# Plain order of an expert pair in a two-layer MoE encoder kernel: gate products, activation, down products

## The chip, the cores and the metric

One core of one Trainium2 chip runs the whole program. The metric is the device time of one execution in microseconds (us). A reading of the profile gives the time of one execution, and the times of three unprofiled executions stand beside it.

## The reference, cut to what matters

Two layers work on 384 tokens of width 1024: 256 of a prompt and 128 of samples. Each layer is a mixer (attention and retention in layer 0, a convolution module in layer 1) and then a mixture of experts (MoE). The change is in the MoE alone. Everything is float32.

```python
def hier_moe(h, w_grp, b_grp, w_rexp, b_rexp, w_gate, w_up, w_down):
    ...
    for g in range(N_GROUPS):
        a = jnp.einsum('nd,edf->nef', x, w_gate[g])
        u = jnp.einsum('nd,edf->nef', x, w_up[g])
        hid = jax.nn.silu(a) * u * gates[:, g, :, None]
        out = out + jnp.einsum('nef,efd->nd', hid, w_down[g]).astype(F32)
```

There are 32 experts (4 groups of 8), each with three 1024 x 256 matrices. A token uses two of them; `gates` is zero elsewhere.

## The kernel before

**Pairs and windows.** The kernel takes the experts two at a time: 16 pairs (`NP`) in each layer. An expert gets a window of 64 tokens (`CAP`), so a pair fills 128 rows. Here no expert has more than 64 tokens and the loop over windows runs once in each layer.

**The weights of a pair.** A pair needs six loads of 1 MiB, numbered q = 6p to 6p + 5. The first four hold the gate and up matrices, the last two the down matrices. A layer has 96 loads, in two halves of 48 (`HALF`). They go into 20 slots in SBUF. `NEEDED` lists the load numbers of a half in the order in which they are loaded. `TURN` gives the slot position of each place in that order: 0 to 19, 0 to 19, then 5 to 12. So place 53, which is the sixth place of the second half, goes to position 5, and that position held place 40 before. `HOLDS` translates a position into a slot of SBUF, layer by layer, and `FREE` lists the slots in the order in which the mixer ahead gives them up; `FIRST` is the order of the first 20 loads that follows from it. I count the loads of a layer from 0 in the order in which they are loaded.

**The queues.** All expert loads are issued by SyncE (SP), in `expert_loads`. Before each load SP waits in `freed` until TensorE (PE) has used what lay in the slot: `gu_done` counts the gate and up products by load, `d_done` counts the down products by pair. SP's queue is in order, so a load that waits holds up all the later ones. GpSimd (POOL) gathers each pair's token rows from HBM (`gather`, into `XGT`) and scatters the results (`scatter`, from `Y` to `outs`). After the last pair SP loads `outs` back (`outs_back`), and VectorE (DVE) adds it to `X` (`add_back`). The result of the last pair isn't scattered: PE multiplies it with the transposed one-hot matrix (`combined`), and DVE adds that too (`add_last`).

**One pair on the engines.** PE makes the gate and up products (`gate_up`, two halves of 8 matmuls, each kept in the trace as two records). ACT applies silu (`silu`), DVE multiplies (`hidden`), PE transposes the result (`hidden_transposed`), ACT copies it to SBUF (`hidden_out`), PE makes the down products (`down`) and ACT scales them into `Y` (`y_out`). Beside that, PE transposes the rows of the next pair (`rows_transposed`), DVE copies them to `XG` (`rows_out`), and PE looks up the indices of the pair after next (`looked_up`).

**The order before.** PE is one pair behind with the down products: gate products of p, the next rows' transposes, a lookup, down products of p - 1, and then the transposes of the hidden values of p. Only the last pair differs: the down products of pair 14 come ahead of the gate products of pair 15, and those of pair 15 follow it. ACT and the loads have the same order, so `NEEDED` lists the gate loads of p ahead of the down loads of p - 1. The transposes for the window after the last pair, and DVE's copy of them, come at the very end of a window.

Of the kernel before, what the change touches and what calls it, by code (L numbers as in the profile page):

```python
# [42 lines left out]
NP = NE // 2  # L43
# [10 lines left out]
PE_TAPS = [r * NSTRIP for r in ROUNDS]  # L54
UNIT = 2048
LO, HI, SLOTS = 6, 12, 20
HOLDS = ((0, 1, 18, 19, 2, 10, 11, 12, 13, 14, 15, 16, 9, 3, 6, 7, 8, 17, 4, 5), (18, 19, 6, 7, 8, 9, 10, 11, 0, 1, 12, 13, 14, 15, 16, 17, 2, 3, 4, 5))
FREE = ((19, 18, 6, 7, 8, 17, 9, 16, 15, 14, 13, 12, 10, 11, 0, 1, 2, 3, 4, 5), (18, 19, 6, 7, 8, 9, 10, 11, 0, 1, 12, 13, 14, 15, 16, 17, 2, 3, 4, 5))
LOADS = 6 * NE // 2
HALF = LOADS // 2  # L60
NEEDED = [q for p in range(HALF // 6 - 1) for q in list(range(6 * p, 6 * p + 4)) + ([6 * p - 2, 6 * p - 1] if p else [])]
NEEDED += [HALF + n for n in (-8, -7, -6, -5, -4, -3, -2, -1)]
SKEW = 5
TURN = [*range(SLOTS), *range(SLOTS), *range(SKEW, SKEW + HALF - 2 * SLOTS)]
FIRST = [[NEEDED[holds.index(n)] for n in free] for holds, free in zip(HOLDS, FREE)]


def turn(q):

    return NEEDED.index(q % HALF)  # L70


def place(q):

    return TURN[turn(q)]


def laps(q):
# [3 lines left out]

def lap(q):

    return TURN[:turn(q)].count(place(q))


def held_before(q):

    n = next(n for n in range(turn(q) - 1, turn(q) - HALF - 1, -1) if TURN[n % HALF] == place(q))  # L90
    return NEEDED[n % HALF] + n // HALF * HALF


UNITS = NP + 2
# [131 lines left out]
def build(nc, a, o):  # L226

    with ExitStack() as ctx:
# [200 lines left out]
        def _(sp):  # L429
# [36 lines left out]

            def last_held(lay, n):

                return NEEDED[max(i for i in range(HALF) if HOLDS[lay][TURN[i]] == n)]

            def outs_back(lay, u):

# [6 lines left out]
            def expert_loads(lay, extra0):  # L479

                b, _ = layer_base(lay, extra0)
                for q in NEEDED[SLOTS:]:
                    freed(b, held_before(q))
                    expert_load(lay, q)
                sp.wait_ge(S("steps_known"), lay + 1)
                n = sp.value_load(NW[0:1, lay:lay + 1], min_val=0, max_val=MAXWIN - 1)
                with sp.Fori(1, n * 2 + 2) as half:
                    for q in NEEDED:
                        freed(b + half * (NP // 2), held_before(q))
                        expert_load(lay, q, half % 2)  # L490
                return n
# [181 lines left out]
        def _(pe):  # L673
# [386 lines left out]
            def moe(lay, extra0):  # L1060
# [145 lines left out]
                with pe.Fori(0, n + 1) as w:  # L1206
                    b, u = b0 + w * NP, u0 + w
                    for p in range(NP):
                        if p == NP - 1:
                            down(b, u, p - 1)  # L1210
                        gate_up(b, u, p, 0)
                        if p == 0:
                            looked_up(b, u, 0, 0, slice(0, 4))
                            looked_up(b, u, 1, 1, slice(0, 4, 3))
                            looked_up(b, u, 2, 2, slice(0, 4))
                        gate_up(b, u, p, 1)
                        if p + 1 < NP:
                            rows_transposed(b, u, p + 1)
                        if p:
                            looked_up(b, u, p + 2, p + 2, slice(0, 4) if p + 2 < NP else slice(1, 3))  # L1220
                        if p == NP - 3:
                            slots_transposed(u)
                        if 1 <= p < NP - 1:
                            down(b, u, p - 1)
                        hidden_transposed(b, p)
                    down(b, u, NP - 1)
                    rows_transposed(b, u, NP)
                combined(b0 + (n * NP + NP), u0 + (n + 1))
                if lay == 0:
                    x_transposed(1)  # L1230
# [102 lines left out]
        def _(act):  # L1333
# [151 lines left out]
            def moe(lay, extra0):  # L1485
                if lay:
                    preload(ACT.Sqrt)
                else:
                    fox_mixed(2)
                act.wait_ge(S("stored"), 16 * (STATE_STORES + lay * CONV_STORES))  # L1490
                gain = 2 * lay + 1
                for t in range(NT):
                    act.wait_ge(S("xt_done"), 2 * NT * lay + 2 * t + 1)
                    q.do(A(HM[:, 0:4, P * t:P * (t + 1)], PS[:, 4, :].rearrange("p (k n) -> p k n", n=P), ACT.Copy),
                         S("hm_act"))
                    act.wait_ge(S("x_mixed"), 2 * NT * lay + 2 * t + 2)
                    square(gain, t, XSQ[:, :])
                    rms(gain, t, t + 1)
                q.do(A(TB[:, :, :, 1], bc(C["tid"], 2, NE), ACT.Copy))
                act.wait_ge(S("rstd_ready"), (NT + 1) * (lay + 1))  # L1500
                q.do(A(TB[:, :, :, 2], bc(norms[:, gain, 6:9], 2, NE), ACT.Copy))
                q.settle()
                q.link(A(stat[:, 12:13], C["eps"], ACT.Copy), S("tb_ready"))
                preload(ACT.Exp)
                act.wait_ge(S("gl_centred"), 2 * lay + 1)
                q.link(A(E4[:, :, :], E4[:, :, :], ACT.Exp), S("gl_exp"))
                act.wait_ge(S("gl_centred"), 2 * lay + 2)
                q.link(A(R8[:, 21:24], R8[:, 18:21], ACT.Exp), S("gl_exp"))
                preload(ACT.Silu)

                def silu(b, u, p):

                    act.wait_ge(S("gu_done"), b * 4 + (4 * p + 4))
                    act.wait_ge(S("idx_read"), u * UNITS + (lay + 2 + p))
                    if p:
                        act.wait_ge(S("hid_ready"), b + p)
                    A(SG[:, :], PS[:, 2 + p % 2, 0:FE], ACT.Silu, scale=SC[:, p, 0:1]).then_inc(S("silu_ready"), 1)  # L1517

                def hidden_out(b, p):

                    act.wait_ge(S("hid_tr"), b + (p + 1))
                    A(HID[:, p % 2, :, :, :].rearrange("p j e n -> p (j e n)"), PS[:, 2 + p % 2, 0:FE], ACT.Copy  # L1522
                      ).then_inc(S("hidT_ready"), 1)

                def y_out(b, u, p):

                    act.wait_ge(S("d_done"), b + (p + 1))
                    act.wait_ge(S("idx_read"), u * UNITS + (lay + 2 + p))
                    if p:
                        act.wait_ge(S(f"scattered{p % 2}"), u * SENT + 16 * ((p + 1) // 2))  # L1530
                    A(Y[:, p % 2, :], PS[:, 4:6, :].rearrange("p a n -> p (a n)"), ACT.Copy,  # L1531
                      scale=SC[:, p, 1:2]).then_inc(S("y_ready"), 1)

                b0, u0 = layer_base(lay, extra0)
                act.wait_ge(S("steps_known"), lay + 1)
                n = act.value_load(NW[0:1, lay:lay + 1], min_val=0, max_val=MAXWIN - 1)
                with act.Fori(0, n + 1) as w:
                    b, u = b0 + w * NP, u0 + w
                    for p in range(NP):
                        if p == NP - 1:  # L1540
                            y_out(b, u, p - 1)
                        silu(b, u, p)
                        if 1 <= p < NP - 1:
                            y_out(b, u, p - 1)
                        hidden_out(b, p)
                    y_out(b, u, NP - 1)
                    for parity in range(2):
                        act.wait_ge(S(f"scattered{parity}"), u * SENT + SENT)
                return n
# [67 lines left out]
        def _(dve):  # L1617
# [312 lines left out]
            def moe(lay, extra0):  # L1930
# [64 lines left out]
                with dve.Fori(0, n + 1) as w:  # L1995
# [4 lines left out]
                    index_out(u, 2, 2, slice(0, 2), slice(0, 2))  # L2000
                    for p in range(NP):
                        hidden(b, p)
                        if p + 1 < NP:
                            rows_out(b, p + 1)
                        if 1 <= p < NP - 2:
                            index_out(u, p + 2, p + 2, slice(0, 2), slice(0, 2))
                        elif p:
                            index_out(u, p + 2, p + 2, slice(1, 2), slice(0, 1))
                        if p == NP - 3:
                            dve.wait_ge(S("gt_tr"), u + 1)  # L2010
                            V.tensor_copy(GT[:, :], PS[:, 6, 0:TOK]).then_inc(S("gt_ready"), 1)
                            V.tensor_scalar(SV[:, :, :], SV[:, :, :], float(-CAP), None, ALU.add).then_inc(S("sv_moved"), 1)
                            dve.wait_ge(S("sv_moved"), u + 1)
                        if p + 1 < NP:
                            onehot(u, p + 3)
                    rows_out(b, NP)

                def add_back(t):

# [176 lines left out]
```

## Time and profile before

| | |
|---|---|
| median of 3 executions | 925.65 us (924.63 to 926.55) |
| the profiled execution | 927.78 us, of which the span shown is 926.0 us |
| PE matmul busy | 863.5 us (93%) |
| DVE, ACT, POOL busy | 337.3 us (36%), 213.6 us (23%), 93.5 us (10%) |
| moved by DMA | 276.91 MB, mean 299 GB/s |
| mean granted TensorE clock | 0.99 of full speed |
| MoE of layer 0 | about 254 to 487 us of the span |
| MoE of layer 1 | about 690 to 923 us of the span |

PE's busy share says little here, since matmuls are pipelined and their ends are modelled. The DMA rate by stretch tells more: the chain that ended last has expert loads and SP's queue in it, with 13% and 8% of the span.

### The profile page before, as it was taken

The page shows a single profiled execution, that of the slowest core. Times are in us where ns is not written, and L with a number is a line of the kernel's source. Part 1 is how long each engine was busy: PE and PEld are TensorE (multiplying, and loading weights), DVE is VectorE, ACT ScalarE, POOL GpSimd, SP SyncE. Part 2 cuts the span into 40 slices and gives each one's busy share as a digit, 9 for nine tenths or more (in the row PEclk, how much of TensorE's full clock was granted, in tenths as well). Part 3 has the DMA queues.
Part 4 walks back from the last instruction along what each step waited for, and adds up shares of the span by engine and source line. Part 5 has one row for each costly group of instructions (what it writes and reads, how often), then busy time and mean ns, then how long its engine had stood idle before and what let it go on. Part 6 is the DMA issues. An engine that isn't in the chain of part 4 may idle for free.

```text
span 926.0 us, 14125 instructions
## 1 busy us (share of the span) xinstructions
PE 863.5 (93%) x5406; PEld 492.9 (53%) x5406; DVE 337.3 (36%) x809; ACT 213.6 (23%) x464; POOL 93.5 (10%) x110
## 2 busy tenths in 40 slices
PE   8999999999999999978778999989999999988775
PEld 6888888888843333322235555447973333333222
DVE  1521653433631111111053689983262111101105
ACT  4322233522211111111123123335121111111010
POOL 1400000000021111101100000000011111111110
PEclk9999999999999999999997999999999999999998
DMA  9972720595889998999999521043559998999995
GB/s 356 414 269 68 213 103 1 219 414 213 345 336 417 405 419 345 419 419 418 419 393 421 201 92 70 23 120 146 204 198 395 418 411 361 395 417 418 420 418 232
DMA packets 49730, 276.91 MB, mean 299 GB/s; under 512 B 11304, under 2 KB 11456, under 8 KB 20920
## 3 DMA queue, kind: packets, MB, share of 16 engines
q1 hardware_dynamic: 35472, 244.94, 65.7%
q0 software_dynamic: 13616, 30.02, 9.4%
q10 hardware_dynamic: 576, 1.05, 0.3%
q8 instruction: 44, 0.72, 0.3%
q14 instruction: 22, 0.18, 0.1%
HBM read 267.62 MB, written 31.66 MB: 323 GB/s over the span
## 4 chain that ended last, share of the span: by engine, by line
PE 66%; DMA 14%; SPq 8%; DVE 7%; issue 2%; ACT 2%; DVEq 0%; ACTq 0%
PE PS L1131 13%; DMA slot<-in_experts 13%; PE PS L700 13%; PE PS L1256 9%; SPq L457 8%; PE PS L1155 7%; PE PS L960 7%; PE PS L937 2%; PE PS L1109 2%; DVE X L1622 2%; PE PS L1275 2%; PE PS L1066 1%; PE PS L1097 1%; DVE YC L2099 1%; DMA HT<-in_x_feat 1%
## 5 line engine op out<-in xcount | busy, mean ns | idle before, releaser
L1131 PE MATMUL PS<-slot,XG 128*64 128x512 f32 x1024 | 233.6, 598 | 28.9 <-DMA slot<-in_experts 28.6
L1131 PEld LDWEIGHTS PS<-slot,XG 128*64 128x64 f32 x1024 | 69.3, 136 | 170.2 <-issue 137.6
L1952 DVE SCALAR_TENSOR_TENSOR hid_by_token<-PS,SC,SG 128x256 f32<-128x256 f32 x32 | 15.5, 484 | 348.5 <-ACT SG L1517 344.7
L700 PE MATMUL PS<-slot,HT 128*128 128x256 f32 x576 | 131.4, 383 | 1.0 <-ACT HT L1357 1.0
L1155 PE MATMUL PS<-slot,HID 128*64 128x512 f32 x512 | 116.6, 597 | 3.5 <-ACT HID L1522 3.5
L700 PEld LDWEIGHTS PS<-slot,HT 128*128 128x128 f32 x576 | 107.3, 190 | 19.2 <-ACT HT L1357 3.3
L1256 PE MATMUL PS<-HC,slot 128*128 128x384 f32 x256 | 88.9, 504 | 1.6 <-DVE HC L2048 1.6
L1256 PEld LDWEIGHTS PS<-HC,slot 128*128 128x128 f32 x256 | 49.0, 195 | 41.7 <-issue 11.8
L1517 ACT ACTIVATE SG<-PS,SC 128x256 f32<-128x256 f32 x32 | 15.2, 475 | 233.1 <-PE PS L1131 233.1
L1531 ACT ACTIVATE Y<-PS,SC 128x1024 f32<-128x1024 f32 x32 | 35.7, 1115 | 139.6 <-PE PS L1155 139.6
L1155 PEld LDWEIGHTS PS<-slot,HID 128*64 128x64 f32 x512 | 33.5, 137 | 60.4 <-issue 53.5
L618 POOL DMA_INDIRECT XGT<-rows,IDX x34 | 34.9, 1025 | 301.2 <-DVE SC L1945 238.5
L1961 DVE TENSOR_TENSOR XG<-PS,small 128x512 f32<-128x512 f32 x68 | 43.7, 682 | 10.6 <-PE PS L1109 10.2
L2099 DVE SCALAR_TENSOR_TENSOR YC<-U,small,YC 128x384 f32<-128x384 f32 x74 | 45.1, 610 | 0.0
L960 PE MATMUL PS<-slot,YC 128*128 128x256 f32 x192 | 42.2, 379 | 0.4 <-ACT YC L1611 0.4
L1109 PEld LDWEIGHTS PS<-cst,XGT 128*128 128x128 f32 x256 | 27.5, 141 | 26.3 <-issue 21.4
L2099 DVE SCALAR_TENSOR_TENSOR YD<-U,small,YD 128x384 f32<-128x384 f32 x66 | 40.2, 610 | 0.0
L960 PEld LDWEIGHTS PS<-slot,YC 128*128 128x128 f32 x192 | 36.2, 190 | 5.8 <-issue 1.0
L626 POOL DMA_INDIRECT outs<-Y,IDX x30 | 30.2, 1008 | 85.1 <-ACT Y L1531 68.3
L1109 PE MATMUL PS<-cst,XGT 128*128 128x128 f32 x256 | 34.9, 279 | 0.2 <-DMA XGT<-rows,IDX 0.2
L1374 ACT ACTIVATE PJ<-PS,norms 128x256 f32<-128x256 f32 x36 | 16.9, 474 | 77.9 <-PE PS L700 77.5
L1275 PE MATMUL PS<-U,DG 32*32 32x384 f32 x736 | 22.5, 505 | 3.0 <-ACT stat L1579 3.0
(308 smaller groups left out, 825.4 us busy)
## 6 DMA issues: line engine op xcount, KB each, us to landing
slot<-in_experts SPq DMA_DIRECT2D x192, 1024.0 KB, 16.1
slot<-in_w_pw SPq DMA_DIRECT2D x12, 1024.0 KB, 9.9
slot<-in_w_in SPq DMA_DIRECT2D x11, 1024.0 KB, 12.1
outs<-slot POOLq DMA_DIRECT2D x12, 512.0 KB, 10.1
slot<-outs SPq DMA_DIRECT2D x6, 1024.0 KB, 8.1
slot<-in_w_out SPq DMA_DIRECT2D x4, 1024.0 KB, 7.3
rows<-X POOLq DMA_DIRECT2D x6, 512.0 KB, 8.6
KTC<-in_k_past POOLq DMA_DIRECT2D x1, 2048.0 KB, 13.8
```

The lines of the kernel that those rows point to most:

```text
L457: sp.dma_start(slot[HOLDS[lay][place(q)]][:, :], experts[bass.ds(half * HALF + (lay * LOADS + q), 1), :, :].rearrange("o p n -> p (o n)")) ...
L618: pool.indirect_dma_start(XGT[:, p % 2, :], None, rows[lay], bass.IndirectOffsetOnAxis(IDX[:, p % NP, 1:2], 0), bounds_check=TOK - 1, oob_ ...
L700: last = mm(PS[:, in_bank(n), 0:UCOL], HT[:, k, P * t:P * (t + 1)], w[:, k, :], start=k == 0, stop=k == KD - 1)
L960: last = mm(PS[:, RING[i % 4], UCOL * (u % 2):UCOL * (u % 2) + UCOL], lhs[:, k, P * t:P * (t + 1)], w[:, k, :], start=k == 0, stop=k == ks ...
L1109: last = nc.tensor.transpose(PS[:, k // 4, P * (k % 4):P * (k % 4 + 1)], XGT[:, p % 2, P * k:P * (k + 1)], ident)
L1131: last = mm(PS[CAP * e:CAP * (e + 1), 2 + p % 2, :], XG[:, p % 2, k, CAP * e:CAP * (e + 1)], w[:, k % 2, e, :], start=k == 0, stop=k == KD ...
L1155: last = mm(PS[CAP * e:CAP * (e + 1), 4 + n, :], HID[:, p % 2, j, e, :], w[:, e, 512 * n:512 * (n + 1)], start=j == 0, stop=j == 1, skip_g ...
L1256: last = mm(PS[:, 2 * (c % 2) + g, 0:TOK], w[:, k, P * cc:P * (cc + 1)], HC[:, k, :], start=k == 0, stop=k == KD - 1)
L1275: last = mm(PS[STRIP * j:STRIP * (j + 1), 4 + i, 0:TOK], DG[rows, c % 2, w, :], U[rows, c, :, w:w + LS], start=m == 0, stop=m == ROUNDS[c] ...
L1531: A(Y[:, p % 2, :], PS[:, 4:6, :].rearrange("p a n -> p (a n)"), ACT.Copy, scale=SC[:, p, 1:2]).then_inc(S("y_ready"), 1)
L1961: V.tensor_tensor(XG[:, p % 2, 4 * h:4 * h + 4, :], PS[:, h, :].rearrange("p (k n) -> p k n", n=P), bc(GC[:, gain, 4 * h:4 * h + 4], 2, P) ...
L2099: ins = V.scalar_tensor_tensor(acc, src, tap, acc, ALU.mult, ALU.add)
```

## The change

PE, ACT and DVE now treat each pair in plain order. On PE these are gate products of p, the transposes of the rows of p + 1, the lookup, the hidden transposes of p and the down products of p. On ACT `y_out` of p follows `hidden_out` of p. The loads go by number, so that `NEEDED` and `turn` are gone, and `HOLDS` of layer 0 is renumbered. For the last pair the row transposes for a following window, and DVE's copy of them, now stand inside the pair and no longer at the end.

```diff
-HOLDS = ((0, 1, 18, 19, 2, 10, 11, 12, 13, 14, 15, 16, 9, 3, 6, 7, 8, 17, 4, 5), (18, 19, 6, 7, 8, 9, 10, 11, 0, 1, 12, 13, 14, 15, 16, 17, 2, 3, 4, 5))
+HOLDS = ((0, 1, 18, 19, 2, 9, 10, 11, 12, 13, 14, 15, 16, 3, 4, 5, 6, 7, 8, 17), (18, 19, 6, 7, 8, 9, 10, 11, 0, 1, 12, 13, 14, 15, 16, 17, 2, 3, 4, 5))
...
-NEEDED = [q for p in range(HALF // 6 - 1) for q in list(range(6 * p, 6 * p + 4)) + ([6 * p - 2, 6 * p - 1] if p else [])]
-NEEDED += [HALF + n for n in (-8, -7, -6, -5, -4, -3, -2, -1)]
...
-FIRST = [[NEEDED[holds.index(n)] for n in free] for holds, free in zip(HOLDS, FREE)]
+FIRST = [[holds.index(n) for n in free] for holds, free in zip(HOLDS, FREE)]
...
-                for q in NEEDED[SLOTS:]:
+                for q in range(SLOTS, HALF):
                     freed(b, held_before(q))
                     expert_load(lay, q)
...
                     for p in range(NP):
-                        if p == NP - 1:
-                            down(b, u, p - 1)
                         gate_up(b, u, p, 0)
...
                         gate_up(b, u, p, 1)
-                        if p + 1 < NP:
-                            rows_transposed(b, u, p + 1)
+                        rows_transposed(b, u, p + 1)
...
-                        if 1 <= p < NP - 1:
-                            down(b, u, p - 1)
                         hidden_transposed(b, p)
-                    down(b, u, NP - 1)
-                    rows_transposed(b, u, NP)
+                        down(b, u, p)
...
                     for p in range(NP):
-                        if p == NP - 1:
-                            y_out(b, u, p - 1)
                         silu(b, u, p)
-                        if 1 <= p < NP - 1:
-                            y_out(b, u, p - 1)
                         hidden_out(b, p)
-                    y_out(b, u, NP - 1)
+                        y_out(b, u, p)
...
                         hidden(b, p)
-                        if p + 1 < NP:
-                            rows_out(b, p + 1)
+                        rows_out(b, p + 1)
...
-                    rows_out(b, NP)
```

On PE, at pair 7 of layer 0, this stands before. L1131 are gate products, L1109 the row transposes, L1097 the lookup, L1155 down products and L1140 the hidden transposes; the first number in a slot's name is its slot in SBUF.

```order
L1131 MATMUL PS<-slot12_69,XG_114 64x512 x4
L1131 MATMUL PS<-slot13_70,XG_114 64x512 x4
L1126 REGISTER_ALU
L1131 MATMUL PS<-slot14_71,XG_114 64x512 x4
L1131 MATMUL PS<-slot15_72,XG_114 64x512 x4
L1109 MATMUL PS<-cst_50,XGT_119 128x128 x8
L1084 REGISTER_ALU
L396 REGISTER_ALU
L1097 MATMUL PS<-TB_130,G_115 64x4 x6
L1155 MATMUL PS<-slot10_67,HID_133 64x512 x4
L1155 MATMUL PS<-slot11_68,HID_133 64x512 x4
L1140 MATMUL PS<-cst_50,hid_by_token_132 128x128 x2
```

And this stands there after the change, from the end of pair 6 to the end of pair 7's gate products and row transposes (here L1123 are gate products, L1101 row transposes, L1132 hidden transposes, L1147 down products).

```order
L1132 MATMUL PS<-cst_50,hid_by_token_132 128x128 x2
L1109 REGISTER_ALU
L1147 MATMUL PS<-slot9_66,HID_133 64x512 x4
L1147 MATMUL PS<-slot10_67,HID_133 64x512 x4
L1118 REGISTER_ALU
L1123 MATMUL PS<-slot11_68,XG_114 64x512 x4
L1123 MATMUL PS<-slot12_69,XG_114 64x512 x4
L1118 REGISTER_ALU
L1123 MATMUL PS<-slot13_70,XG_114 64x512 x4
L1123 MATMUL PS<-slot14_71,XG_114 64x512 x4
L1101 MATMUL PS<-cst_50,XGT_119 128x128 x8
```

The down products of pair 6 used to follow pair 7's gate products and now precede them. They use the loads of places 40 and 41, and those slots take places 53 and 54 next.

On DVE, at the end of layer 0's MoE, this stands before: the last `hidden`, the last index, the copy of the rows for a following window (XG), and then the additions to X.

```order
L1952 SCALAR_TENSOR_TENSOR hid_by_token_132<-PS,SC_136,SG_116 128x256
L1942 REGISTER_ALU
L1944 TENSOR_SCALAR IDX_135<-PS 128x1
L1945 COPY SC_136<-PS 128x1
L1958 REGISTER_ALU
L1960 REGISTER_ALU
L1961 TENSOR_TENSOR XG_114<-PS,small_51 128x512
L1960 REGISTER_ALU
L1961 TENSOR_TENSOR XG_114<-PS,small_51 128x512
```

After the change it is this.

```order
L1934 SCALAR_TENSOR_TENSOR hid_by_token_132<-PS,SC_136,SG_116 128x256
L1940 REGISTER_ALU
L1942 REGISTER_ALU
L1943 TENSOR_TENSOR XG_114<-PS,small_51 128x512
L1942 REGISTER_ALU
L1943 TENSOR_TENSOR XG_114<-PS,small_51 128x512
L1924 REGISTER_ALU
L1926 TENSOR_SCALAR IDX_135<-PS 128x1
L1927 COPY SC_136<-PS 128x1
```

The two copies have moved ahead of the last index. What PE does for them, the row transposes, stood behind the last down products and now stands between the last gate products and the last hidden transposes.

## Rows read from the trace of the kernel before

**Rows 1.** Windows: PE, PEld, DVE, ACT, POOL busy us, granted clock, DMA share, GB/s.
```profile
350.00:360.00 10.00, 10.00 (x56) 3.71 (x52) 0.41 (x2) 1.87 (x3) 1.94 (x2) 1.00 0.78 280
780.00:790.00 10.00, 10.00 (x62) 3.90 (x60) 2.28 (x6) 1.86 (x3) 2.01 (x2) 1.00 0.64 238
400.00:460.00 60.00, 49.21 (x255) 16.51 (x252) 8.97 (x25) 8.10 (x12) 8.30 (x9) 1.00 1.02 419
```
**Rows 2.** DMA queue of the loads, 270 to 345 us, then 705 to 780 us.
```profile
q1 hardware_dynamic: 3958, 28.83, 93.1%
...
q1 hardware_dynamic: 4022, 29.29, 94.2%
```
**Rows 3.** The chain that ended last: start us, us, what.
```profile
265.31 7.09 PE PS L1131 x32
...
273.87 3.48 PE PS L1155 x16
277.73 7.02 PE PS L1131 x32
...
348.03 3.48 PE PS L1155 x16
...
700.25 7.09 PE PS L1131 x32
...
782.87 3.49 PE PS L1155 x16
```
**Rows 4.** Timeline of SP: start us, us, line, operation.
```profile
256.74 5.45 SPq L457 DMA_DIRECT2D slot<-in_experts  x3
...
351.70 3.33 SPq L457 DMA_DIRECT2D slot<-in_experts  x6
...
786.54 4.33 SPq L457 DMA_DIRECT2D slot<-in_experts  x6
```
**Rows 5.** Timeline around the first pair and the last pair of layer 0.
```profile
264.71 0.44 PE L1140 MATMUL PS<-cst,hid_by_token 128*128 128x128 f32 x2 [0.15 <-DVE hid_by_token L1952]
...
466.45 1.94 PE L1131 MATMUL PS<-slot,XG 128*64 128x512 f32 x8 [0.77 <-DMA slot<-in_experts]
...
469.62 0.44 PE L1140 MATMUL PS<-cst,hid_by_token 128*128 128x128 f32 x2 [0.93 <-DVE hid_by_token L1952]
470.09 0.38 ACT L1522 ACTIVATE HID<-PS 128x256 f32<-128x256 f32 x1 [1.05 <-PE PS L1140]
470.53 3.65 PE L1155 MATMUL PS<-slot,HID 128*64 128x512 f32 x16 [0.47 <-ACT HID L1522]
```
**Rows 6.** Timeline behind the last pair of layer 0, then of layer 1.
```profile
474.81 1.29 DVE L1961 TENSOR_TENSOR XG<-PS,small 128x512 f32<-128x512 f32 x2 [5.11 <-PE PS L1109]
...
475.57 5.41 PE L1176 MATMUL PS<-Y,GT 128*128 128x512 f32 x12 [0.36 <-ACT Y L1531]
476.01 4.99 DVE L1622 TENSOR_TENSOR X<-X,slot 128x1024 f32<-128x1024 f32 x4
...
911.59 4.99 DVE L1622 TENSOR_TENSOR X<-X,slot 128x1024 f32<-128x1024 f32 x4
```
**Rows 7.** SP's loads of `outs`: first issue in each layer (timeline), their DMA lines.
```profile
468.70 1.42 SPq L476 DMA_DIRECT2D slot<-outs  x3
slot<-outs SPq DMA_DIRECT2D x1, 1024.0 KB, 5.3
slot<-outs SPq DMA_DIRECT2D x1, 1024.0 KB, 7.5
...
903.02 1.41 SPq L476 DMA_DIRECT2D slot<-outs  x3
slot<-outs SPq DMA_DIRECT2D x1, 1024.0 KB, 6.5
```
**Rows 8.** DMA issues of the page: the scatters, count, median us to landing.
```profile
outs<-Y,IDX POOLq DMA_INDIRECT x32, 8.0
```

More of the change, by code:

```diff
@@ L60 @@
 HALF = LOADS // 2
-NEEDED = [q for p in range(HALF // 6 - 1) for q in list(range(6 * p, 6 * p + 4)) + ([6 * p - 2, 6 * p - 1] if p else [])]
-NEEDED += [HALF + n for n in (-8, -7, -6, -5, -4, -3, -2, -1)]
 SKEW = 5
 TURN = [*range(SLOTS), *range(SLOTS), *range(SKEW, SKEW + HALF - 2 * SLOTS)]
-FIRST = [[NEEDED[holds.index(n)] for n in free] for holds, free in zip(HOLDS, FREE)]
-def turn(q):
-    return NEEDED.index(q % HALF)
+FIRST = [[holds.index(n) for n in free] for holds, free in zip(HOLDS, FREE)]
 def place(q):
-    return TURN[turn(q)]
+    return TURN[q % HALF]
 def laps(q):
@@ L83, in lap @@
 def lap(q):
-    return TURN[:turn(q)].count(place(q))
+    return TURN[:q % HALF].count(place(q))
 def held_before(q):
-    n = next(n for n in range(turn(q) - 1, turn(q) - HALF - 1, -1) if TURN[n % HALF] == place(q))
-    return NEEDED[n % HALF] + n // HALF * HALF
+    return next(n for n in range(q - 1, q - HALF - 1, -1) if place(n) == place(q))
 UNITS = NP + 2
@@ L467, in last_held @@
             def last_held(lay, n):
-                return NEEDED[max(i for i in range(HALF) if HOLDS[lay][TURN[i]] == n)]
+                return max(q for q in range(HALF) if HOLDS[lay][place(q)] == n)
             def outs_back(lay, u):
@@ L487, in expert_loads @@
                 with sp.Fori(1, n * 2 + 2) as half:
-                    for q in NEEDED:
+                    for q in range(HALF):
                         freed(b + half * (NP // 2), held_before(q))
```

## The prediction, on record before the run

> **What bounds the kernel now.** I read the rate of the DMA engines by stretch first. In the second half of layer 0's MoE it stands at 419 GB/s with a DMA share of 1.02, while PE is busy for 49 of 60 us [rows 1]: the loads set the pace there, and PE waits for them. The same holds in layer 1. In the first half PE has a lead of 20 loads and never waits for one. Its pace is even: from the down products at 273.87 us to those at 348.03 us it makes six pairs in 74.2 us, 12.36 us a pair [rows 3]. The loads are slower. The queue of the loads moved 28.83 MB in 75 us, so that a load of 1.0486 MB takes 2.73 us and a pair's six take 16.4 us [rows 2]. In layer 1 it is 2.69 us and 16.1 us [rows 2].
>
> A stage bound by loads ends earlier only if the stream starts earlier, has fewer holes, or if less stands behind it. So I looked for holes. There is one in each layer: 350 to 360 us moved only 280 GB/s and 780 to 790 us only 238 GB/s [rows 1]. Against 418 GB/s that is 10 x (1 - 280/418) = 3.3 us and 4.3 us without data. In both cases SP ends the hole with a burst of six issues, at 351.70 and 786.54 us [rows 4], right behind down products that end at 348.03 + 3.48 = 351.5 us and 782.87 + 3.49 = 786.4 us [rows 3]. These are the down products of pair 6. The first load of the burst is load 53; its slot held load 40, a down load of pair 6. The distance is 13 loads there, where elsewhere it is 15 to 28. So the hole is made by the slot order, and by the fact that PE does the down products of pair 6 only after pair 7's gate products.
>
> **The change part by part.** Term 1, PE's pace. Nothing is added to PE's work, but a wait is exposed. Between the hidden transposes and what follows there stood gate products, which waited for nothing; these came 0.38 us after the end of the down products (277.73 less 273.87 + 3.48) [rows 3]. Now the down products follow, and they need ACT's copy. The last pair already runs this way: transposes at 469.62, copy at 470.09, down products at 470.53 us, which is 0.91 us from start to start [rows 5]. Silu and DVE's product lie under the row transposes and the lookup, since the hidden transposes could start 469.62 - 468.39 = 1.2 us behind the last gate product [rows 5], and the other two take longer than that (the down products start 1.5 us behind gate products that end at 272.40) [rows 3]. So a pair takes 12.36 + 0.91 - 0.38 = 12.9 us. This is still 3.3 us under the loads' 16.1 to 16.4 us, and the cover for it is the lead of 20 loads: no cost of its own.
>
> Term 2, when down slots come free. The first hidden transposes start at 264.71 us [rows 5]; down 0 then starts at 265.6 and ends at 269.2 us. Down p ends at 269.2 + 12.9 p. For pair 6 that is 346.7 us, against 351.5 now. Layer 1's second pair starts 434.94 us later (700.25 less 265.31) [rows 3], which gives 704.2 us for down 0 and 781.6 us for down 6, against 786.4. The slot comes 4.8 us earlier, and the holes are 3.3 and 4.3 us: both close. I take 3.3 + 4.3 = 7.6 us. The Trainium skill ("DMA: Bandwidth & Descriptors", "Specifications") gives about 358 GB/s as a core's HBM limit. The trace runs at 419 GB/s here, so I go by the trace; with 358 as the full rate the holes would be 2.2 and 3.4 us and the total gain 8.7 us.
>
> Term 3, new holes. In plain order loads 24 and 25 wait for down 0, and loads 43 and 44 for down 4; before they waited for gate products and for the down products of pair 3 and gate products. Let a load's data start 1 us behind its issue (my estimate). The stream then wanted load 53 at 351.7 + 1 - 3.3 = 349.4 us, load 43 ten loads before, at 322.1, and load 24 at 270.2 us. After the change these can flow at 320.8 + 1 = 321.8 and at 270.2 us: on the edge. In layer 1 load 53 was wanted at 783.2, load 43 at 756.4 and load 24 at 705.3 us, and they can flow at 756.8 and 705.2 us: 0.4 us late. Bounds: nothing if the issue is faster than that, and 1.6 us a layer if the first four refills, issued from 256.74 us [rows 4], flow at full rate (257.7 + 4 x 2.73 = 268.6, against 270.2). I charge 0.5 and 0.4 us, and as a delay of the stream they are one charge a layer. Terms 2 and 3 give 6.7 us.
>
> Term 4, behind the last load. DVE now copies the rows of a following window (1.29 us) behind PE's last work, and only then, at 476.01 us, adds what SP loads back [rows 6]. But the first block lands at 468.70 + 5.3 = 474.0 us and the second at about 469.13 + 7.5 = 476.6 us [rows 7], the second being issued 0.43 us after the first. With the copy moved into the pair, the four additions run as 474.0 to 476.5 and 476.6 to 479.1 us and end 1.9 us before today's 481.0 [rows 6]. In layer 1 the first block lands at 903.02 + 6.5 = 909.5 us [rows 7]; the additions end at 914.5 us and not at 911.59 + 4.99 = 916.6 [rows 6]: 2.1 us. Bounds: nothing if the landings move as late as DVE, and 2.0 and 2.1 us if DVE starts the moment the first block is there. On PE the row transposes (1.1 us) now stand ahead of the last hidden transposes. Together with the lookup they take 1.5 us where the chain needs 1.2, so the last down products come 0.3 us later; the last products with Y start at 475.9 instead of 475.57 us and DVE wants the first of them at 479.1. That is hidden. Term 4 is 4.0 us.
>
> Nothing else counts. The first 20 loads are the same number in the same slots and land before the first gate product. ACT's order has `y_out` directly behind the down products, ahead of the next silu, which is 7 us away. SP passes through the same number of waits. POOL's gathers and scatters keep their order; a scatter's data is ready some 12 us earlier.
>
> Sum: 7.6 - 0.9 + 4.0 = 10.7 us. The profiled execution took 927.78 us (span 926.0 and 1.8 around it), 2.1 us above the median. Its successor should show 917.1 us, and the median goes from 925.65 to 914.9, say 915.0 us. A measurement of this kernel tells 0.2%, 1.9 us, from no change.
>
> **The rivals.** (a) The holes close only by half: the gap of 13 loads is still the tightest place, and 0.4 us in layer 1 are no margin. For it speaks that three places (24, 43, 53) come within a microsecond of the stream. Against it, 4.8 us gained on a wait of 3.3. With half of 7.6 and the 0.9 charge the gain is 6.9, so 918.8 us, and 921 us with 1.6 us a layer lost as well. Chance 0.16.
>
> (b) The tails give nothing, since the landings or the last products hold DVE. For it speaks that in layer 1 all three blocks come only within DVE's reach of the end. Gain 6.7 us, 918.9 us. Chance 0.12.
>
> (c) Nothing to be measured: the stream's rate, not its holes, gives back what the holes cost, because packets only run more densely with the scatters. Against it, the rate stands at 413 to 419 GB/s on either side of each hole. 925 us. Chance 0.05.
>
> (d) Slower, by ACT's queue. `y_out` of p waits until the scatter of p - 2 has landed, and it now stands ahead of silu of p + 1, so that a late scatter stops PE's whole chain. POOL issues the scatter of p - 2 behind a gather, by my estimate 4.5 us after pair p - 1's gate products (the lookup at 1.0, DVE's index and the gather behind it). With 8.0 us to landing [rows 8] it is there 12.5 us after them, and `y_out` of p wants it at 12.9 + 5.9 = 18.8 us. It decides when a landing takes over 14.3 us, and beyond that each microsecond is one more on a pair. At 14.0 us a pair down 6 ends at 353.2 us, each layer loses 2 us and the tails' 4.0 are used up. At 15 us a pair it is 8 us a layer: 925.65 + 16 - 4 = 938 us. Chance 0.05.
>
> (e) Slower, by PE's clock. PE now stops in every pair, where it ran from 265 to 390 us without a stop. Where it stops far more today, the granted clock is 1.00, which is 2.4 GHz, with 11 us idle in 60 [rows 1]. The Trainium skill ("TensorE: Matmul & The Clock Gate", "Why this matters for your kernels") warns that idle gaps between bursts bring the clock down; new gaps of 0.5 us are far shorter than those today. At 1.2 GHz a pair would take 25.8 us. If pairs 0 to 6 ran so, load 53 would come 85 us later, some 1090 us in all. Chance 0.02.
>
> **How the numbers follow.** My forecast, 911.5 to 918 us, has 0.60. Cases (a) and (b) lie at 918 to 921 us on the same side. The range is 911.5 to 920.5: it leaves out the slow cases and no change (0.12), and some 0.08 at the two ends. Faster: 0.60 + 0.16 + 0.12 = 0.88. Same 0.05, slower 0.07.
>
> **What the profile would show.** Right: about 12.9 us between pairs in the first half, down products of pair 6 that end at 347 and 4.7 us earlier in layer 1, no stretch of 10 us under 360 GB/s between 265 and 440 us, PE waiting for loads only from pair 13 on instead of pair 10, and DVE's additions to X starting before PE's last down products end. Wrong: a hole at about 268 us or 320 us, a pair of 13.5 us or more, silu waiting behind `y_out`, or additions to X that start as late after the last load as today.

## The result, and the profile after

The changed kernel takes 916.55 us (median of 4, 914.61 to 918.94), the kernel before 926.1 us (median of 4, 924.63 to 927.42). The ratio is 0.9898, with a 95% interval of 0.9867 to 0.993: 9.4 us faster, by at least 6.5. Ratios here and below are taken over each kernel's undisturbed executions, and the only one left out is an execution of E6 that took 2812.07 us, for which no trace shows a cause. The forecast was 915.0 us in a range of 911.5 to 920.5. The profiled execution took 918.94 us with a span of 917.2, which is 8.8 us under its predecessor, where I had written 10.7.

The windows that answer to [rows 1] (PE, PEld, DVE, ACT, POOL busy us, granted clock, DMA share, GB/s):

```profile
350.00:360.00 10.00, 9.53 (x60) 4.01 (x58) 2.27 (x6) 1.56 (x3) 2.01 (x2) 1.00 1.02 425
780.00:790.00 10.00, 9.53 (x58) 3.88 (x56) 2.27 (x6) 0.95 (x3) 2.02 (x2) 1.00 1.01 420
400.00:460.00 60.00, 52.95 (x293) 19.97 (x291) 9.77 (x26) 7.90 (x12) 9.27 (x9) 1.00 1.02 417
```

280 and 238 GB/s have become 425 and 420, and 770 to 780 us, where layer 1's hole would now lie, moves 419: both holes are gone. Two windows ahead of layer 0's hole changed as well. First the kernel before, then the changed one:

```profile
310.00:320.00 10.00, 10.00 (x62) 3.71 (x61) 2.28 (x6) 1.57 (x3) 2.02 (x2) 1.00 0.99 387
340.00:350.00 10.00, 10.00 (x62) 3.94 (x60) 2.28 (x6) 1.16 (x3) 1.09 (x2) 1.00 0.93 381
```

```profile
310.00:320.00 10.00, 9.53 (x59) 3.84 (x56) 2.28 (x6) 0.86 (x2) 1.71 (x2) 1.00 1.03 420
340.00:350.00 10.00, 9.45 (x58) 4.07 (x58) 2.28 (x6) 1.97 (x3) 2.02 (x2) 1.00 1.02 418
```

So the kernel before lost another 0.7 and 0.9 us there, which the prediction didn't count. Next comes the chain that ended last, at the first pair and at pair 6 (down products in L1147, gate products in L1123, row transposes in L1101, hidden transposes in L1132):

```profile
265.60 3.65 PE PS L1147 x16
269.26 6.87 PE PS L1123 x32
276.12 1.02 PE PS L1101 x8
277.15 0.45 PE PS L1089 x12
277.60 0.38 PE PS L1132 x2
278.00 0.39 ACT HID L1508
278.44 3.65 PE PS L1147 x16
282.09 6.87 PE PS L1123 x32
...
342.69 3.65 PE PS L1147 x16
346.34 6.87 PE PS L1123 x32
```

From 269.26 to 282.09 a pair takes 12.83 us, and 12.36 before [rows 3]. Pair 6's down products end at 346.3 us, not at 351.5. The timeline of SP shows load 53 issued right behind them, at 346.52 us, where it stood at 351.70 [rows 4]:

```profile
346.52 5.48 SPq L449 DMA_DIRECT2D slot<-in_experts  x5
```

The end of layer 0's MoE, in the timeline (XG is the copy that was moved, L468 are the loads of `outs`):

```profile
462.23 1.94 PE L1123 MATMUL PS<-slot,XG 128*64 128x512 f32 x8 [1.07 <-DMA slot<-in_experts]
...
465.26 1.28 DVE L1943 TENSOR_TENSOR XG<-PS,small 128x512 f32<-128x512 f32 x2
...
466.48 3.65 PE L1147 MATMUL PS<-slot,HID 128*64 128x512 f32 x16 [0.47 <-ACT HID L1508]
...
466.57 1.42 SPq L468 DMA_DIRECT2D slot<-outs  x3
...
471.44 2.48 DVE L1604 TENSOR_TENSOR X<-X,slot 128x1024 f32<-128x1024 f32 x2 [4.77 <-DMA slot<-outs]
```

The copy is out of DVE's way, as it should be. But DVE now waits 4.77 us for the landing of `outs`. SP asks for `outs` 4.3 us after the last gate products begin (462.23); before it was 2.3 us (468.70 less 466.45) [rows 5, 7]. The end of layer 1:

```profile
893.23 1.94 PE L1123 MATMUL PS<-slot,XG 128*64 128x512 f32 x8 [1.10 <-DMA slot<-in_experts]
...
896.60 1.41 SPq L468 DMA_DIRECT2D slot<-outs  x3
...
902.59 2.48 DVE L1604 TENSOR_TENSOR X<-X,slot 128x1024 f32<-128x1024 f32 x2 [4.92 <-DMA slot<-outs]
```

What `outs` waited for is in the chain that ended last. In layer 0 it no longer goes through the last gate products. It runs from the down products of pair 14 (L1147) over their scatter (`outs<-Y,IDX`) to SP's request and the landing of the second block:

```profile
450.95 3.67 PE PS L1147 x16
...
456.95 9.60 DMA outs<-Y,IDX
466.57 0.40 SPq L468
467.01 7.03 DMA slot<-outs
474.13 1.24 DVE X L1604
```

### The profile page after: what moved, and what is told of

It is laid out like the page before. It is cut to its first block, busy times and chain, and to the rows that moved or that the text cites. A ratio compares the mean times of both kernels' runs of the same rounds, so it can differ in the third digit from the quotient of the medians.

```text
span 917.2 us, 14121 instructions
## 1 busy us (share of the span) xinstructions
PE 859.1 (94%) x5406; PEld 498.6 (54%) x5406; DVE 337.2 (37%) x809; ACT 216.6 (24%) x464; POOL 93.4 (10%) x110
## 4 chain that ended last, share of the span: by engine, by line
PE 65%; SPq 12%; DMA 11%; DVE 7%; ACT 3%; issue 2%; DVEq 0%; ACTq 0%; POOLq 0%
PE PS L692 13%; PE PS L1123 12%; SPq L449 11%; PE PS L1242 9%; PE PS L1147 7%; PE PS L952 7%; DMA slot<-in_experts 6%; PE PS L929 2%; DMA outs<-Y,IDX 2%; DVE X L1604 2%; PE PS L1101 2%; PE PS L1261 2%; DMA slot<-outs 2%; PE PS L1058 1%; PE PS L1089 1%
## 5 line engine op out<-in xcount | busy, mean ns | idle before, releaser
L1123 PE MATMUL PS<-slot,XG 128*64 128x512 f32 x1024 | 229.2, 594 | 12.7 <-DMA slot<-in_experts 12.7
L1123 PEld LDWEIGHTS PS<-slot,XG 128*64 128x64 f32 x1024 | 72.6, 137 | 160.7 <-issue 143.8
L1147 PE MATMUL PS<-slot,HID 128*64 128x512 f32 x512 | 116.9, 598 | 15.4 <-ACT HID L1508 15.4
L1147 PEld LDWEIGHTS PS<-slot,HID 128*64 128x64 f32 x512 | 34.0, 136 | 77.8 <-issue 57.0
L1101 PEld LDWEIGHTS PS<-cst,XGT 128*128 128x128 f32 x256 | 27.5, 141 | 26.0 <-issue 23.5
L1101 PE MATMUL PS<-cst,XGT 128*128 128x128 f32 x256 | 35.0, 280 | 0.0
```

Source lines behind the costliest of these rows:

```text
L1101: last = nc.tensor.transpose(PS[:, k // 4, P * (k % 4):P * (k % 4 + 1)], XGT[:, p % 2, P * k:P * (k + 1)], ident)
L1123: last = mm(PS[CAP * e:CAP * (e + 1), 2 + p % 2, :], XG[:, p % 2, k, CAP * e:CAP * (e + 1)], w[:, k % 2, e, :], start=k == 0, stop=k == KD ...
L1147: last = mm(PS[CAP * e:CAP * (e + 1), 4 + n, :], HID[:, p % 2, j, e, :], w[:, e, 512 * n:512 * (n + 1)], start=j == 0, stop=j == 1, skip_g ...
```

## The experiments

Theory A: the holes are waits for slots, and PE's order of the pair closed them. Theory B: the additions at the end are held by `outs`, whose loads wait for the scatter of pair 14, and the moved copy gives next to nothing. Rival C: the order of the loads did it. Rival D: the hole is a stall of the chip's own.

**E1, the changed kernel again.** 

> The changed kernel once more, as the measure for the runs beside it. All theories: 0.990 of the kernel before, 916 to 917 us. Theory A (release): the down products of pair 6 end near 346.3 us and no 10 us stretch from 265 to 440 us falls under 360 GB/s. Theory B (end): the first block of outs lands some 9.2 us after the last gate load of a layer is there, and DVE's additions to X begin on that landing in both layers.

918.08 us (6 runs), ratio 0.9894 (0.987 to 0.9918). Pair 6's down products end at 346.25 us, no 10 us window from 270 to 440 us moves less than 370 GB/s, and DVE's additions wait for the landing of `outs` in both layers, 9.2 and 8.8 us after the last gate products begin. Both parts hold.

**E2, plain engines, old load order.** PE, ACT and DVE as in the change; `NEEDED`, `turn` and `HOLDS` as before.

> PE, ACT and DVE in plain order, but the loads in the old order (gate loads of p ahead of the down loads of p - 1). Theory A, that the holes closed because PE frees pair 6's down slots earlier: down 6 ends near 346.5 us, the holes at 350 and 780 us are closed, the time is that of the changed kernel within 1.5 us, 915 to 918 us. Rival C, that the gain comes from loading by number: the holes stay or most of the 9.4 us is lost, 922 us or more.

924.71 us (10 runs), ratio 0.9974 (0.9955 to 0.9994). By time the rival was right, and the time is 6.7 us above the range that I gave theory A. By place it wasn't: the old holes did close, with 418 GB/s from 350 to 360 us. But there are new ones. From its first refill (the first load that takes over the slot of an earlier load of the layer) E2 moves 26.71 MB in 70 us and the changed kernel 27.66; in layer 1 it is 26.52 and 27.59 MB. At 418 GB/s that is 2.3 and 2.6 us. The largest is from 270 to 280 us, with 317 GB/s against 365: in the old list place 24 waits for gate products of pair 1, which plain PE makes only after the down products of pair 0. The rest of the loss, some 2.5 us of 7.4, is at the end. The timeline of E2 from 448 us (L1155 down, L1131 gate products):

```profile
448.09 1.94 PE L1155 MATMUL PS<-slot,HID 128*64 128x512 f32 x8 [0.46 <-DMA slot<-in_experts]
449.85 7.04 PE L1131 MATMUL PS<-slot,XG 128*64 128x512 f32 x32
459.28 3.65 PE L1155 MATMUL PS<-slot,HID 128*64 128x512 f32 x16 [0.55 <-ACT HID L1516]
462.76 7.04 PE L1131 MATMUL PS<-slot,XG 128*64 128x512 f32 x32
472.11 3.65 PE L1155 MATMUL PS<-slot,HID 128*64 128x512 f32 x16 [0.47 <-ACT HID L1516]
```

The down loads of pair 13 come behind the gate loads of pair 14, and plain PE wants them first. When they are there at 448 us, all of pair 14's and most of pair 15's gate work is still to be done at PE's own pace. The last down products end at 475.8 us, against 470.1 in the changed kernel.

**E3, the copy back at the end.**

```diff
-                        rows_transposed(b, u, p + 1)
+                        if p + 1 < NP:
+                            rows_transposed(b, u, p + 1)
...
                         down(b, u, p)
+                    rows_transposed(b, u, NP)
...
-                        rows_out(b, p + 1)
+                        if p + 1 < NP:
+                            rows_out(b, p + 1)
...
+                    rows_out(b, NP)
```

> The changed kernel with the row transposes for a following window, and DVE's copy of them, back behind the last down products. My prediction's term 4 (DVE's copy held up the additions, 1.9 and 2.1 us): 4 us slower than the changed kernel, near 920.5 us. Theory B (the landing of outs holds them since the change, and the copy is hidden): within 0.5 us of the changed kernel, additions start 0 to 0.4 us later against the last gate load.

916.65 us (4 runs), ratio 0.9897 (0.9866 to 0.9928); E1 on the same chip has 0.9894. My term 4 falls: 4 us more would have been 0.994. The timeline of DVE in both layers:

```profile
470.12 1.29 DVE L1945 TENSOR_TENSOR XG<-PS,small 128x512 f32<-128x512 f32 x2 [5.11 <-PE PS L1101]
471.33 2.48 DVE L1606 TENSOR_TENSOR X<-X,slot 128x1024 f32<-128x1024 f32 x2
...
898.87 1.29 DVE L1945 TENSOR_TENSOR XG<-PS,small 128x512 f32<-128x512 f32 x2 [5.11 <-PE PS L1101]
900.08 2.47 DVE L1606 TENSOR_TENSOR X<-X,slot 128x1024 f32<-128x1024 f32 x2
```

Its last gate products begin at 461.77 and 890.52 us. The additions begin 9.56 us after them in both layers, exactly as in the kernel before (476.01 - 466.45) [rows 5, 6]. In the changed kernel it is 9.21 and 9.36 us. So the start of the additions moves by 0.35 and 0.2 us. Their end moves less, since the second block is late: in layer 0 the first four are done 14.4 us after the last gate products begin, and 14.6 us in E3 and in the kernel before. From the last gate products of layer 1 to the end of the span it is 24.0 us in all three.

**E4, the old order for pairs 13 and 14.** Built on E2, with the changed kernel's `HOLDS`:

```diff
+NEEDED = [*range(HALF - 14), *range(HALF - 12, HALF - 8), HALF - 14, HALF - 13, *range(HALF - 8, HALF)]
...
+                        if p == NP - 2:
+                            down(b, u, p - 1)
                         hidden_transposed(b, p)
-                        down(b, u, p)
+                        if p != NP - 3:
+                            down(b, u, p)
```

and the same for `y_out`.

> Plain order for pairs 0 to 12 and 15, the old order for pairs 13 and 14 on PE and ACT, with the gate loads of pair 14 ahead of the down loads of pair 13 (in both halves of the load list). Theory B, that the scatter of pair 14 comes too late in plain order and holds outs back: SP's first load of outs is issued about 2.2 us after the last gate products begin (changed kernel: 4.3 and 3.4 us after them in layers 0 and 1), DVE's additions begin 1.5 to 1.9 us earlier against them in each layer, 913 to 915 us. If another thing binds the end, such as the rate of the three blocks, it is 916 to 917 us as the changed kernel.

917.78 us (6 runs), ratio 0.9894 (0.9864 to 0.9923): no gain over the changed kernel, and above the 913 to 915 us that I expected. The relation that I forecast is there, but not for the reason that I gave. The timeline in layer 0:

```profile
464.72 1.94 PE L1130 MATMUL PS<-slot,XG 128*64 128x512 f32 x8 [0.57 <-DMA slot<-in_experts]
...
467.15 1.42 SPq L475 DMA_DIRECT2D slot<-outs  x3
...
472.51 1.23 DVE L1617 TENSOR_TENSOR X<-X,slot 128x1024 f32<-128x1024 f32 x1 [3.36 <-DMA slot<-outs]
```

SP asks for `outs` 2.4 us after the last gate products begin, and DVE starts 7.8 us after them. But these begin later themselves. From the first refill (258.16 us here, 256.72 in the changed kernel) it is 206.6 us, against 205.5 there and 206.1 in E1; from the first refill to the additions 214.4 and 214.7. Counted so, the scatter of pair 14 isn't any earlier: POOL issues it at 458.53 us here and at 456.95 in the changed kernel, 200.4 and 200.2 us after the first refill. It lands in 8.6 us and not 9.6, so SP asks for `outs` about 0.9 us sooner; the rest of what looks like a gain is that the gate products are late. The windows (columns as above) show what was traded. First the changed kernel, then E4:

```profile
465.00:467.00 2.00, 1.53 (x20) 0.87 (x20) 1.67 (x5) 0.38 (x1) 0.00 (x0) 1.00 0.42 172
467.00:468.00 1.00, 1.00 (x8) 0.39 (x6) 0.00 (x0) 0.00 (x0) 0.46 (x1) 1.00 0.55 66
```

```profile
467.00:469.00 2.00, 1.53 (x23) 1.10 (x20) 1.66 (x4) 0.69 (x2) 0.00 (x0) 1.00 0.65 195
```

Ahead of `outs` the changed kernel has a gap of 2 x (1 - 172/418) + (1 - 66/418) = 2.0 us; E4 has 1.1. More flows ahead of the last gate products in E4: 84.64 MB from 257.4 us on, against 84.33 MB from 256 us on in the changed kernel, or 0.7 us at 418 GB/s. Of these 0.31 MB, 0.09 are on the queue of the gathers and scatters, so pair 14's scatter, which here has more time to flow ahead of the last gate load, is at most a part of it; no run isolates it.

**E5, old engines, loads by number.** With the changed kernel's `HOLDS`.

```diff
-NEEDED = [q for p in range(HALF // 6 - 1) for q in list(range(6 * p, 6 * p + 4)) + ([6 * p - 2, 6 * p - 1] if p else [])]
-NEEDED += [HALF + n for n in (-8, -7, -6, -5, -4, -3, -2, -1)]
+NEEDED = list(range(HALF))
```

> The old order on PE, ACT and DVE, but the loads by number. Theory A (PE's order sets the release, the order of loads doesn't): down 6 still ends near 351.5 us, both holes stay at 3 to 4 us, 925 to 928 us. Rival C (the order of the loads is what gained): holes gone or smaller, 920 us or less.

935.38 us (4 runs), ratio 1.0106 (1.0075 to 1.0136): slower than the kernel before. Rival C is out as the sole cause, though E2 shows that the loads' order is needed too. My own expectation missed as well: the late hole did go, but because a bigger one came first. The windows:

```profile
268.00:272.00 4.00, 4.00 (x22) 1.34 (x18) 0.00 (x0) 0.00 (x0) 0.00 (x0) 1.00 0.58 230
272.00:280.00 8.00, 8.00 (x54) 3.26 (x52) 2.27 (x6) 1.86 (x3) 1.01 (x1) 1.00 0.24 63
...
350.00:360.00 10.00, 10.00 (x54) 3.67 (x52) 0.39 (x1) 1.87 (x3) 1.96 (x2) 1.00 1.02 418
```

Load 24 waits for down 0, which old PE does behind pair 1's gate products; they end at 277.5 us. 8.6 us are lost there, and the stream is so late from then on that load 53 finds its slot free.

**E6 to E8, the place of the extra laps.** `SKEW` shifts the eight positions that a half uses a third time; `HOLDS` swaps two slots along with it.

```diff
-SKEW = 5
+SKEW = 6
```

> The kernel before with SKEW 6 in place of 5: the eight extra loads of a half go one position further on, so that load 54 and not load 53 is the first to wait for pair 6's down products, and loads 40 and 41 wait for those of pair 3 (distances 14 and 14 in place of 15 and 13). Theory A: the hole at 350 us goes, a small one of 1.5 to 2 us appears near 314 and 749 us; net 4 us faster than before, near 922 us. Rival D, that the hole is a stall of the chip (HBM or queue) at the change of halves and not a wait for a slot: the hole stays in its place and the time is 926 us.

922.38 us (5 runs), ratio 0.9948 (0.993 to 0.9966): 4.8 us faster than before, by the place of the extra laps alone. Windows at 315 and at the old hole:

```profile
310.00:320.00 10.00, 10.00 (x62) 3.71 (x61) 2.28 (x6) 1.57 (x3) 2.02 (x2) 1.00 0.80 295
350.00:360.00 10.00, 10.00 (x56) 3.71 (x52) 0.42 (x2) 1.86 (x3) 1.93 (x2) 1.00 1.02 418
```

The hole at 350 us is gone, and the one at 310 to 320 us has grown from 387 to 295 GB/s, that is from 0.7 to 10 x (1 - 295/418) = 2.9 us; I had expected 1.5 to 2. In layer 1 it is the same, with 414 GB/s from 780 to 790 us and 295 from 740 to 750. The hole goes where the wait for a slot goes. Rival D is out.

> The changed kernel with SKEW 6: loads 42 and 43 now wait for pair 4's down products and are wanted at 319.5 us, where these end at 320.6. Theory A: a hole of 2 to 2.5 us near 320 us and the same near 750 us, 4 to 5 us slower than the changed kernel, near 921 us. Rival D: no change, 916 to 917 us.

920.77 us (10 runs), ratio 0.9944 (0.9924 to 0.9963). The window at the new hole of layer 0:

```profile
316.00:326.00 10.00, 9.53 (x51) 3.36 (x50) 1.67 (x5) 1.50 (x2) 2.02 (x2) 1.00 0.95 339
```

The whole of it lies between 310 and 326 us, where E7 moves 355 GB/s and the changed kernel 418; in layer 1 it is 361 and 414 GB/s from 740 to 760 us. The holes are 16 x (1 - 355/418) = 2.4 us and 20 x (1 - 361/418) = 2.7 us. Against E1's 0.9894 (another chip, each against the kernel before beside it) the kernel is 0.5% slower, some 4.6 us. As expected.

> The changed kernel with SKEW 4: load 52 in place of 53 waits for pair 6's down products (distance 12). Theory A: load 52 is wanted at about 346.5 us and can flow at 347.5, a hole of about 1 us a layer, 1 to 3 us slower than the changed kernel, 917.5 to 919.5 us. Rival D: no change.

919.37 us (4 runs), ratio 0.9924 (0.9903 to 0.9945); 0.3% above E1, but the two intervals overlap, so the time alone doesn't tell it from the changed kernel. The hole does. From 345 to 351 us it moves 367 GB/s and the changed kernel 416: 0.7 us in layer 0, where I had expected about 1. Pair 6's down products are hardly a microsecond ahead of the stream, and load 53 is the first that can wait for them.

**E9, small matmuls against a falling clock.** 4 + 9 + 3 matmuls of 128 columns whose results nothing reads, at three places between layer 0's MoE and the convolution, for instance

```diff
                     x_transposed(2)
+                    for _ in range(9):
+                        mm(PS[:, 3, TOK:TOK + P], cst[:, 0:P], cst[:, 0:P], start=True, stop=True, skip_group_check=True)
```

> The changed kernel with 16 small matmuls on PE whose results nothing reads: 4 behind layer 0's last products with Y, 9 while PE waits for the third tile of X, 3 ahead of the matmuls for the row scales. Theory E: the granted clock fell to 0.5 at 484 us because PE was idle for half of 476 to 484 us, and the first convolution matmuls then ran slow until 494 us; with the small matmuls the clock stays at 1.00 (or falls later and for less), and the convolution stage, from its first to its last glu product, takes 109.1 us and not 112.1: 3 us faster than the changed kernel, near 914 us, and less scatter between executions. Rival: the clock falls anyhow, as the small matmuls don't fill enough: 917 to 918 us, or 0.5 us slower by what they delay.

917.72 us (6 runs), ratio 0.9895 (0.9868 to 0.9921). The clock did what was expected; the median didn't. The trace shows what became of the time. Layer 1's first refill is issued at 683.86 us, 3.5 us before the changed kernel's 687.32, but its last gate products begin at 892.30 us, only 0.9 us before 893.23. Between the two 85.26 MB flowed, against 84.40, and 0.86 MB are 2.1 us at 418 GB/s: the mixer was done earlier, and more of the loads was still to come.

**E10, the changed kernel beside E9.** 

> The changed kernel, beside e9 on the same chip: 0.990 of the kernel before, 916 to 918 us, executions spread over some 4 us, the shorter ones with a mean clock of 0.995 and the longer ones with 0.991.

916.62 us (6 runs, 916.57 to 917.35), ratio 0.9887 (0.9868 to 0.9905). The spread that I expected was not there. Windows of the changed kernel, of E9 and of E10, from 484 to 492 us:

```profile
484.00:492.00 8.00, 5.61 (x18) 3.52 (x16) 5.34 (x14) 0.87 (x3) 0.00 (x0) 0.52 1.02 422
```

```profile
484.00:492.00 8.00, 6.21 (x32) 4.38 (x30) 5.82 (x15) 1.11 (x4) 0.00 (x0) 1.00 1.01 421
```

```profile
484.00:492.00 8.00, 6.45 (x27) 5.20 (x27) 4.83 (x13) 1.61 (x4) 0.00 (x0) 0.80 1.02 422
```

And the first convolution matmuls in the chain (64 records), in the same order:

```profile
488.66 23.81 PE PS L1242 x64
```

```profile
488.18 20.88 PE PS L1248 x64
```

```profile
489.17 20.88 PE PS L1242 x64
```

The granted clock at 0.52 costs 2.9 us there. E9 avoids it, but E10, without small matmuls, had its fall earlier and was back at the full clock before these began. In E10 too the gain shrinks in layer 1, from 2.5 us at the first refill (684.81) to 1.3 at the last gate products (891.89). No version beats the changed kernel beyond the intervals.

## Why the prediction was right, step by step

**Term 1, PE's pace: right.** 12.83 us a pair against 12.9 forecast, down 0 ending at 269.3 against 269.2, down 6 at 346.3 against 346.7. The exposed copy was read from the last pair before, the only one that ran in plain order already.

**Term 2, the holes close: right and shown, but undersized.** They are gone in the profile, E6 moves the hole with the slot order alone, and E7 and E8 open new ones: 2.4 and 0.7 us in layer 0, where the same two lines (when a down product ends, when the stream wants its slot) gave 2 to 2.5 and 1. E6's was 2.9 and not 1.5 to 2. The reading of the holes was narrow: one window of 10 us each. Layer 0 had 0.7 us more from 310 to 320 us and 0.9 us from 340 to 350. With 381 GB/s ahead of the hole (and 407 behind it in layer 1), my sentence in rival (c) that the rate stands at 413 to 419 on either side was a wrong reading. The assumption that a load's data start 1 us behind its issue fits the trace: load 53 is issued at 351.70 us, and the first packets of that queue come between 352.5 and 352.7.

**Term 3, new holes: too small, within its bound.** In layer 0, 260 to 270 and 270 to 280 us moved 388 and 413 GB/s before and 381 and 365 after, which is 1.3 us; I charged 0.5 and bounded it at 1.6.

**Terms 2 and 3 together were too small.** I forecast 2.8 and 3.9 us. The last gate products begin 4.2 us earlier in layer 0 (466.45 to 462.23) and 8.8 in layer 1 (902.02 to 893.23). Layer 1's first refill is 4.3 us early (691.65 to 687.32), which leaves 4.5 for layer 1. That is 8.7 and not 6.7 us. Besides the holes that I hadn't counted, less flows ahead of these products: from 256 us on 84.67 MB before and 84.33 MB after, in layer 1 from its first refill on 84.77 and 84.40 MB, which is 0.8 and 0.9 us at 418 GB/s. For layer 0 that makes 3.3 + 1.6 - 1.3 + 0.8 = 4.4 us, against 4.2 measured. E4 agrees: with the old order of the last pairs 84.64 MB flow, and these products come 0.5 to 1.1 us later, counted from the first refill.

**Term 4, the copy: wrong.** 4.0 us forecast, 0.2 us measured in layer 0 and nothing in layer 1. The step that failed is "the first block lands at 474.0", which I held fixed against the last loads. SP waits for the scatter of pair 14 before it asks for `outs`, and in plain order pair 14's gate loads come two loads later in the list. Counted from the layer's first refill, the last gate products came 4.2 and 4.5 us earlier, but that scatter was issued only 3.0 and 3.1 us earlier (before at 459.98 and 895.09, after at 456.95 and 887.64) and took 9.6 and 9.0 us to land, where it had taken about 8.7 and 7.9. So SP's request moved by 2.1 us in both layers. Two of the signs that I had named turned against the forecast here: the additions start nearly as late after the last load as before, and at 471.44 us they are behind the end of PE's last down products (466.48 + 3.65 = 470.1), not ahead of it. I had named "nothing, if the landings move as late as DVE" as the lower bound and rival (b) for this case; it came true while the loads gained 2 us more than I had summed. Two errors of about +2 and -4 us partly cancel. That 916.6 us lies so near to 915.0 is in part luck; the mechanism of the holes isn't.

**The rivals.** (a) and (c) didn't occur. (b) did, as a mechanism. (d): from 262 to 470 us ACT waits for PE alone and never for a scatter; PE's waits from 262 to 460 us are 7.2 us for ACT's copy in 15 pairs, the 0.48 us a pair that term 1 had priced, and 5.1 us for loads. (e): from 262 to 470 us the granted clock stays at 1.00, which is 2.4 GHz. It wasn't out of reach: in E2, where PE waits up to 3.2 us at a time for down loads, it was 0.78 from 390 to 400 us and 0.84 from 430 to 440, while the loads kept their 420 and 414 GB/s.

**That the change would need both of its halves** I had not said. The engines' order alone gives 0.3%, the loads' order alone costs 1.1%, both together gain 1.0%.

## What to carry to other kernels

In a stage bound by loads, look for windows in which the rate falls, and ask which slot the first load behind the gap waited for; the price is the time by which the stream wants the slot before its user is done, and both can be written as lines over the pairs. Load order, use order and slot release are one design: here the engines' order alone gained 0.3%, the loads' order alone cost 1.1%, and both together gained 1.0%. Read a hole from its edges and not from one round window, or part of it is missed. Work that is moved off the end pays only if the next thing in line, here a landing, isn't late itself, so move it on paper together with all that precedes it. And count both from a common event, such as the first refill: counted from the last gate products, E4 looked like a success.

## What the runs showed of the hardware that I had not expected

**The same matmuls take 3 us more or less by where the clock falls.** Behind layer 0's MoE PE is idle for about half of 476 to 484 us. In one execution the granted clock was 0.52 from 484 to 492 us, in another of the same kernel (E10) 0.55 from 480 to 484, 0.60 from 484 to 488 and 1.00 after. The 64 records of matmuls that follow took 23.81 us in the one and 20.88 in the other. The Trainium skill ("TensorE: Matmul & The Clock Gate", "Why this matters for your kernels") warns of idle gaps between bursts; the rows agree that the fall comes after one. A change of 3 us at this place can't be told from this effect by one profile. The time of the whole kernel needn't follow: the six executions of E10 have mean clocks from 0.991 to 0.996 and lie within 0.8 us.

**One core draws 417 to 420 GB/s from HBM for 60 us at a time,** beside gathers and scatters. The Trainium skill ("DMA: Bandwidth & Descriptors", "Specifications") names about 358 GB/s per core as the limit of HBM, the half of what a stack gives to two cores; here, with one core at work, the measured number is 17% above it.
